# Feed-forward first stages of a two-block transformer: one 512-column product for both parts of h, sums in two banks

## The chip, the cores and the metric

The kernel runs on one core of one Trainium2 chip. The metric is the device time of one execution in microseconds. Before the change three runs gave 1700.32, 1704.14 and 1704.25 us; their median, 1704.14 us, is the time before.

## The reference, cut to what matters

x is 256 tokens by 1024 features. A first block (two attentions, then a gated feed-forward with a convolution, here called the stage "o") is followed by two layers of a second block. Each layer has a feed-forward, a mixer of three attentions, and a second feed-forward, all with modulated norms. The four feed-forwards of the two layers are what the change is about:

```
def swiglu(h, w_gate, w_up, w_down):
    return (jax.nn.silu(h @ w_gate) * (h @ w_up)) @ w_down

for l in range(DEPTH_2):                      # 2 layers
    h = modulate(x, norm_pre[l, 0], mod[:, 0, 0], mod[:, 0, 1])
    x = residual_add(x, swiglu(h, ffn_w_gate[l, 0], ffn_w_up[l, 0], ffn_w_down[l, 0]), ...)
    ...                                       # token mixer
    h = modulate(x, norm_pre[l, 2], mod[:, 2, 0], mod[:, 2, 1])
    x = residual_add(x, swiglu(h, ffn_w_gate[l, 1], ffn_w_up[l, 1], ffn_w_down[l, 1]), ...)
```

w_gate and w_up are 1024 by 2816, w_down is 2816 by 1024. All data is float32.

## The kernel before

Every product is made of float32r parts. A weight w is split into hi (a rounded copy) and lo (w minus hi), an activation h into h_hi and h_lo, and `three` (L516) adds up hi times h_hi, hi times h_lo and lo times h_hi in PSUM; lo times h_lo is left out.

The weights come in 269 chunks of 128 x 2048 (1 MB), in an order fixed beforehand. SP loads each into one of three raw buffers once the lo split of three chunks before is done (`load_chunk`, L426). ACT writes hi (`split`, L916), DVE writes lo (L1307). There are three hi/lo slots, and a fourth from the end of one mixer to the start of the next, so that in the changed stages the split of chunk k+4 stands behind the products of chunk k on ACT and on DVE (`split_behind`, L933 and L1313). A second list, 192 rows of modulation weights (ada, 0.5 MB each), is loaded by SP into three buffers and reduced on DVE, one row behind most chunks (`ada`, L1328).

A first stage of a feed-forward ("up0" and "up2" of layers 0 and 1) has 22 chunks (FT). A chunk k holds two tiles of 128 output features, j = 0 for the gate and j = 1 for the up weights, each with eight tiles t of 128 input features. Chunks 0 and 1 are done by `fm_first` (L542), which starts while h is still being made. Chunks 2 to 21 are done by `fm` (L529): 48 products with a stationary 128x128 piece of the weights and a moving 128x256 piece of h. Both j go to one bank of the pair lin, columns 0 to 255 and 256 to 511; banks alternate by chunk, and a bank is written again when DVE has signalled taken_v for the chunk two before.

```
for j in range(2):
    for t in range(KT):
        b = slice((j * KT + t) * P, (j * KT + t + 1) * P)
        ins = three(out[:, j * SEQ:(j + 1) * SEQ], hi[s][:, b], lo[s][:, b], h_hi[:, t, :],
                    h_lo[:, t, :], t == 0, t == KT - 1)
```

ACT takes Silu of the gate half out of the bank into a work tile (`silu_gate`, L1158), then makes the next hi split. DVE multiplies that with the up half (L1655; this frees the bank), makes the lo split, and writes act_hi (a rounding copy, L1647) and act_lo (L1649) with drains between (`swiglu`, L1651; `second_of`, L1645); then comes the ada row. work[2] and work[3] serve in turn.

The second stage of a feed-forward (`down`, L729) multiplies act with w_down in 11 chunks of 24 products with 512 columns (L694), into the four att banks. `into_h` (L752) turns x through pt, nps and two att banks before each first stage. Stage o.up of the first block has the same products as up0 (`fm`), but a convolution on ACT and DVE (`conv_glu`, L1666), act_hi on ACT (L1199) and act_lo on DVE (L1682); its order of work is written out by hand as well.

PSUM has eight banks here: lin 0 and 1, att 2 to 5, pt 6, nps 7.

Of the kernel before, what the change touches and what calls it, by code (L numbers as in the profile page):

```python
# [7 lines left out]
F32 = mybir.dt.float32  # L8
# [4 lines left out]
P = 128  # L13
# [186 lines left out]
def program(nc, d, known):  # L200

    with ExitStack() as ctx:
        def sb(name, shape, dt=F32, scope=ctx):
            return scope.enter_context(nc.sbuf_tensor(name, shape, dt))
# [6 lines left out]

        x = sb("x", [P, 2, D])
        sb("h_shift", [P, 72])
        h_parts = [sb("h_hi", [P, KT * SEQ + IN_STEP], F32R)]
        ada_out = sb("ada_out", [P, ADA_ALL])
        eps = sb("eps", [P, 1])
        h_parts.append(sb("h_lo", [P, KT * SEQ + IN_STEP], F32R))
        sb("work_shift", [P, 16])
        h_hi, h_lo = (h[:, 0:KT * SEQ].rearrange("p (t n) -> p t n", t=KT) for h in h_parts)
        m_hi, m_lo = (h[:, IN_STEP:].rearrange("p (t n) -> p t n", t=KT) for h in h_parts)  # L220
# [51 lines left out]
        with ExitStack() as scope:  # L272
            sb("under_fourth", [P, 56 * 256 + FOURTH_SHIFT], F32, scope)
            hi.append(sb("hi3", [P, CH], F32R, scope))
            lo.append(sb("lo3", [P, CH], F32R, scope))

        lin = ctx.enter_context(nc.psum_tensor("lin", [P, 2, 512], F32))
        att = ctx.enter_context(nc.psum_tensor("att", [P, 4, 512], F32))
        pt = ctx.enter_context(nc.psum_tensor("pt", [P, 512], F32))
# [6 lines left out]
        def signal(name):  # L286
            signals[name] = Signal(ctx.enter_context(nc.semaphore(name)), name, known)
            return signals[name]
# [27 lines left out]
                                                   signal("sp"), signal("d"))  # L316
        s_part_v, s_h, s_x = signal("part_v"), signal("h"), signal("x_made")
        s_z, s_scaled, s_h_hi_v = signal("z"), signal("scaled"), signal("h_hi_v")
        s_glu, s_half_mean = signal("glu"), signal("half_mean")
        s_act, s_taps, s_merged, s_rot, s_lat = (signal("act_made"), signal("taps"), signal("merged"), signal("rot"),  # L320
                                                 signal("lat_made"))
        s_lat_lo, s_halved = signal("lat_lo"), signal("halved")
# [86 lines left out]

        def bank_of(unit):  # L410
            return att[:, 2, :] if unit == WIDE else lin[:, BANK[unit], :]

        def ada_slot(h):

# [98 lines left out]
        def _(eng):  # L513
# [15 lines left out]
            def fm(name):  # L529

                c = AT[name]
                eng.wait_ge(*s_lo.at(c))
                out = free_bank((c, 0))
                s = SLOT[c]
                for j in range(2):
                    for t in range(KT):
                        b = slice((j * KT + t) * P, (j * KT + t + 1) * P)
                        ins = three(out[:, j * SEQ:(j + 1) * SEQ], hi[s][:, b], lo[s][:, b], h_hi[:, t, :],
                                    h_lo[:, t, :], t == 0, t == KT - 1)
                ins.then_inc(*s_mm.up((c, 0), c))  # L540

            def fm_first(tag, *names):  # L542
# [349 lines left out]
            for l in map(str, range(LAYERS)):  # L892
                into_h(l + ".pre0", flat_f, 8 if l == "0" else 5, 8 if l == "0" else 4)
                fm_first(l + ".pre0", f"{l}.up0.0", f"{l}.up0.1")
                for k in range(2, FT):
                    fm(f"{l}.up0.{k}")
                down(l + ".down0")
                into_h(l + ".pre1", flat_f, 5, 4)
                fm_first(l + ".pre1", f"{l}.moba.q0", f"{l}.moba.k0")
                tm(f"{l}.moba.v0")  # L900
                fm(f"{l}.moba.q1")
                eng.wait_ge(*s_dcon_in.at("dcon"))
                mixing(l, MIX_HEADS, MIX_SLOTS, {11: lambda: latent_sums(l)})
                out_proj(l)
                into_h(l + ".pre2", rb[:, 0:8, :], 5, 4)
                fm_first(l + ".pre2", f"{l}.up2.0", f"{l}.up2.1")
                for k in range(2, FT):
                    fm(f"{l}.up2.{k}")
                down(l + ".down2")


# [1 line left out]
        def _(eng):  # L913
# [19 lines left out]
            def split_behind(name):  # L933

                for c in SPLIT_BEHIND.get(AT[name], []):
                    if SLOT_BEFORE[c] == AT[name]:
                        split(c)
# [191 lines left out]
            def mixing(l, heads, before, slots, early, first, late):  # L1129
                n = len(heads)  # L1130
                last = 1 if l == "o" else 2
                for s in range(len(slots) + 1):
# [22 lines left out]
                    for f in late.get(s, []):  # L1155
                        f()

            def silu_gate(stage, k):  # L1158
                c = AT[f"{stage}.{k}"]
                eng.wait_ge(*s_mm.at((c, 0)))  # L1160
                act(work[2 + k % 2][:, 0:SEQ], lin[:, BANK[(c, 0)], 0:SEQ], ACT.Silu).then_inc(*s_gated.up((stage, k)))  # L1161

            def down(stage):

# [31 lines left out]
            h_first("norm2", 24, "o.1", 8)  # L1196
            split_behind("o.out.2")
            split_behind("o.out.3")
            def act_first(k):  # L1199
                eng.wait_ge(*s_glu.at(k))  # L1200
                act(act_hi[:, k, :], work[2 + k % 2][:, SEQ:2 * SEQ], ACT.Copy).then_inc(*s_act_hi.up(k))

            for k in range(FT):
                c = AT[f"o.up.{k}"]
                eng.wait_ge(*s_mm.at((c, 0)))
                for j in range(2):
                    at = PCOL["conv"].start + 8 * k + 4 * j
                    ins = act(work[k % 2][:, j * SEQ:(j + 1) * SEQ], bank_of((c, 0))[:, j * SEQ:(j + 1) * SEQ],
                              ACT.Identity, bias=par[:, at + 3:at + 4], scale=par[:, at + 1:at + 2])
                ins.then_inc(*s_conved.up(k))  # L1210
                if k:
                    act_first(k - 1)
                split_behind(NAMES[c])
                eng.wait_ge(*s_taps.at(k))
                act(work[2 + k % 2][:, 0:SEQ], work[k % 2][:, SEQ:2 * SEQ], ACT.Gelu_apprx_tanh).then_inc(
                    *s_gated.up(("o.up", k)))
            eng.wait_ge(*s_cond_b_in.at(1))
            act(cs[:], cs[:], ACT.Silu).then_inc(*s_silu.up(1))
            act_first(FT - 1)
            log_exp()  # L1220
            down("o.down")
            factor_of_x("norm3", "down", 0)
# [4 lines left out]
            for l in map(str, range(LAYERS)):  # L1227
# [2 lines left out]
                split_behind("o.down.10" if l == "0" else "0.down2.10")  # L1230
                for k in range(FT):
                    silu_gate(l + ".up0", k)
                    split_behind(f"{l}.up0.{k}")

                log_exp()
                down(l + ".down0")
# [50 lines left out]
                split_behind(f"{l}.out.3")  # L1287
                for k in range(FT):
                    silu_gate(l + ".up2", k)
                    split_behind(f"{l}.up2.{k}")  # L1290
                log_exp()
                down(l + ".down2")
                if l == "0":
# [8 lines left out]
        def _(eng):  # L1302
# [10 lines left out]
            def split_behind(name):  # L1313

                for c in SPLIT_BEHIND.get(AT[name], []):
                    if SLOT_BEFORE[c] == AT[name]:
                        split(c)
# [324 lines left out]
                        o_second(l, h + 1)  # L1642
                    ada(c)

            def second_of(k, stage, a):  # L1645

                ve.tensor_copy(act_hi[:, k, :], a)  # L1647
                ve.drain()
                tt(act_lo[:, k, :], a, act_hi[:, k, :].bitcast(F32), ALU.subtract).then_inc(*s_act.up((stage, k)))  # L1649

            def swiglu(stage, to, k):  # L1651
                c = AT[f"{stage}.{k}"]
                w = work[2 + k % 2]
                eng.wait_ge(*s_gated.at((stage, k)))
                tt(w[:, SEQ:2 * SEQ], w[:, 0:SEQ], lin[:, BANK[(c, 0)], SEQ:2 * SEQ], ALU.mult).then_inc(  # L1655
                    *s_taken_v.up((c, 0)))
                split_behind(NAMES[c])
                ve.drain()
                second_of(k, to, w[:, SEQ:2 * SEQ])
                ada(c)  # L1660

            def conv_glu(k):
                c = AT[f"o.up.{k}"]
                eng.wait_ge(*s_conved.at(k))
                for j in (1, 0):
                    at = PCOL["conv"].start + 8 * k + 4 * j  # L1666
                    u = work[k % 2][:, j * SEQ:(j + 1) * SEQ]
                    p = bank_of((c, 0))[:, j * SEQ:(j + 1) * SEQ]
                    stt(u[:, 1:SEQ], p[:, 0:SEQ - 1], par[:, at:at + 1], u[:, 1:SEQ], ALU.mult, ALU.add)
                    ve.drain()  # L1670
                    ins = stt(u[:, 0:SEQ - 1], p[:, 1:SEQ], par[:, at + 2:at + 3], u[:, 0:SEQ - 1], ALU.mult, ALU.add)  # L1671
                    ins.then_inc(*(s_taps.up(k) if j else s_taken_v.up((c, 0))))
                split_behind(NAMES[c])
                if k:
                    act_second(k - 1)
                ve.drain()  # L1676
                eng.wait_ge(*s_gated.at(("o.up", k)))
                w = work[2 + k % 2]
                tt(w[:, SEQ:2 * SEQ], w[:, 0:SEQ], work[k % 2][:, 0:SEQ], ALU.mult).then_inc(*s_glu.up(k))
                ada(c)  # L1680

            def act_second(k):  # L1682

                eng.wait_ge(*s_act_hi.at(k))
                tt(act_lo[:, k, :], work[2 + k % 2][:, SEQ:2 * SEQ], act_hi[:, k, :].bitcast(F32),
                   ALU.subtract).then_inc(*s_act.up(("o.down", k)))

            eng.wait_ge(*s_silu.at(0))
            for i, h in enumerate(START_ORDER):
# [33 lines left out]
            for k in range(FT):  # L1723
                conv_glu(k)
                if k == 15:
                    gate_of(40, "down")
            act_second(FT - 1)
            for k in range(FD - 1):
                if k < FD - 2:
                    split_behind(f"o.down.{k}")  # L1730
# [27 lines left out]
            for l in map(str, range(LAYERS)):  # L1758
# [2 lines left out]
                split_behind("o.down.10" if l == "0" else "0.down2.10")  # L1761
                for k in range(FT):
                    swiglu(l + ".up0", l + ".down0", k)
                layer_post(l, 0)
                for k in range(FD - 1):
                    c = AT[f"{l}.down0.{k}"]
# [29 lines left out]
                split_behind(f"{l}.out.3")  # L1796
                for k in range(FT):
                    swiglu(l + ".up2", l + ".down2", k)
                layer_post(l, 2)
                for k in range(FD - 1):  # L1800
                    c = AT[f"{l}.down2.{k}"]
# [206 lines left out]
```

## Time and profile before

| | |
|---|---|
| median of three runs | 1704.14 us |
| the profiled execution | 1706.34 us |
| its span, first to last instruction | 1704.5 us |
| mean granted clock of TensorE | 0.997 of full speed |
| instructions | 29606, of them 12344 products |

PE is TensorE's products, PEld its weight loads, DVE VectorE, ACT ScalarE, POOL GpSimd, SP the engine that issues most DMAs. "SPq" is a queue, "lin", "att", "work" and the like are the program's names, L with a number is a line of the kernel before. Spans of products overlap, so the time from one start to the next, not the shown length, is what a product costs in a stream; some product records can be missing. "x945" is a number of instructions, "<-" in brackets names what an engine waited for.

### The profile page before, as it was taken

The page shows a single profiled execution, that of the slowest core. Times are in us where ns is not written, and L with a number is a line of the kernel's source. Part 1 is how long each engine was busy: PE and PEld are TensorE (multiplying, and loading weights), DVE is VectorE, ACT ScalarE, POOL GpSimd, SP SyncE. Part 2 cuts the span into 40 slices and gives each one's busy share as a digit, 9 for nine tenths or more (in the row PEclk, how much of TensorE's full clock was granted, in tenths as well). Part 3 has the DMA queues.
Part 4 walks back from the last instruction along what each step waited for, and adds up shares of the span by engine and source line. Part 5 has one row for each costly group of instructions (what it writes and reads, how often), then busy time and mean ns, then how long its engine had stood idle before and what let it go on. Part 6 is the DMA issues. An engine that isn't in the chain of part 4 may idle for free.

```text
span 1704.5 us, 29606 instructions
## 1 busy us (share of the span) xinstructions
PE 1661.0 (97%) x12344; PEld 1551.7 (91%) x12344; DVE 1266.7 (74%) x1852; ACT 873.3 (51%) x1214; POOL 21.7 (1%) x39
## 2 busy tenths in 40 slices
PE   3999999998999999999999999999999999999998
PEld 3999899987999899989989998999899989989997
DVE  7777889977877677776878775877677776878553
ACT  4565466653534355676373434533355676473432
POOL 0000000000000000000000000000000000000000
PEclk9999999999999999999999999999999999999999
DMA  9878756777677744756548786687945856547542
GB/s 378 314 259 249 275 195 213 203 293 280 258 292 276 287 169 184 223 178 232 207 177 296 272 220 261 227 292 270 289 170 183 220 181 233 210 174 259 196 167 96
DMA packets 71078, 398.80 MB, mean 234 GB/s; under 512 B 8224, under 2 KB 8736, under 8 KB 36384
## 3 DMA queue, kind: packets, MB, share of 16 engines
q1 hardware_dynamic: 67968, 387.43, 65.1%
q0 software_dynamic: 2976, 9.47, 1.6%
q8 instruction: 98, 1.61, 0.4%
q14 instruction: 36, 0.29, 0.0%
HBM read 395.79 MB, written 1.08 MB: 233 GB/s over the span
## 4 chain that ended last, share of the span: by engine, by line
PE 79%; DVE 7%; ACT 5%; DMA 4%; DVEq 3%; issue 1%; SPq 1%; ACTq 0%
PE lin L517 18%; PE lin L518 17%; PE lin L519 17%; PE att L694 15%; DVE lo L1310 4%; ACT hi L921 3%; PE att L801 2%; PE lin L557 1%; DMA raw<-in_w 1%; PE lin L559 1%; PE lin L567 1%; DMA ada_w<-in_ada 1%; DVEq L1676 1%; PE att L851 1%; DMA ada_s<-in_ada 1%
## 5 line engine op out<-in xcount | busy, mean ns | idle before, releaser
L1310 DVE TENSOR_TENSOR lo<-raw,hi 128x2048 fp32r<-128x2048 f32 x269 | 615.6, 2291 | 253.1 <-ACT hi L921 252.4
L517 PE MATMUL lin<-h_hi,hi 128*128 128x256 f32 x2448 | 688.5, 281 | 1.3 <-DVE work L1671 0.8
L518 PE MATMUL lin<-h_lo,hi 128*128 128x256 f32 x2448 | 683.8, 279 | 0.0
L519 PE MATMUL lin<-h_hi,lo 128*128 128x256 f32 x2448 | 682.5, 279 | 0.0
L921 ACT ACTIVATE hi<-raw 128x2048 fp32r<-128x2048 f32 x269 | 513.5, 1912 | 194.8 <-PE att L694 91.4
L517 PEld LDWEIGHTS lin<-h_hi,hi 128*128 128x128 f32 x2448 | 460.0, 188 | 4.0 <-issue 3.8
L518 PEld LDWEIGHTS lin<-h_lo,hi 128*128 128x128 f32 x2448 | 460.3, 188 | 0.1
L519 PEld LDWEIGHTS lin<-h_hi,lo 128*128 128x128 f32 x2448 | 460.1, 188 | 0.0
L1323 DVE CUSTOM_DVE_ANT_0 ada_w<-ada_w,cs 128x1024 f32<-128x1024 f32 x179 | 218.0, 1219 | 18.8 <-DMA ada_w<-in_ada 18.7
L1161 ACT ACTIVATE work<-lin 128x256 f32<-128x256 f32 x88 | 33.9, 386 | 269.4 <-PE lin L519 268.2
L694 PE MATMUL att<-hi,act_hi 128*128 128x512 f32 x440 | 138.8, 389 | 0.0
L694 PE MATMUL att<-lo,act_hi 128*128 128x512 f32 x440 | 138.7, 389 | 0.0
L694 PE MATMUL att<-hi,act_lo 128*128 128x512 f32 x440 | 138.7, 389 | 0.0
L694 PEld LDWEIGHTS att<-lo,act_hi 128*128 128x128 f32 x440 | 82.6, 188 | 17.2
L694 PEld LDWEIGHTS att<-hi,act_lo 128*128 128x128 f32 x440 | 82.6, 188 | 17.2
L694 PEld LDWEIGHTS att<-hi,act_hi 128*128 128x128 f32 x440 | 82.2, 188 | 16.8
L517 PE MATMUL lin<-br_hi,hi 128*128 128x256 f32 x224 | 63.4, 283 | 0.1
L518 PE MATMUL lin<-br_lo,hi 128*128 128x256 f32 x224 | 62.5, 279 | 0.0
L519 PE MATMUL lin<-br_hi,lo 128*128 128x256 f32 x224 | 62.5, 279 | 0.0
L557 PE MATMUL lin<-h_hi,hi 128*128 128x256 f32 x224 | 53.4, 282 | 1.1 <-ACT h_hi L1006 1.1
L517 PE MATMUL lin<-hi,h_hi 128*128 128x256 f32 x192 | 54.2, 283 | 0.0
L519 PE MATMUL lin<-hi,h_lo 128*128 128x256 f32 x192 | 53.9, 281 | 0.0
(291 smaller groups left out, 2023.7 us busy)
## 6 DMA issues: line engine op xcount, KB each, us to landing
raw<-in_w SPq DMA_DIRECT2D x269, 1024.0 KB, 4.9
ada_w<-in_ada SPq DMA_DIRECT2D x179, 512.0 KB, 5.4
ada_s<-in_ada SPq DMA_DIRECT2D x13, 512.0 KB, 15.3
bias<-in_bias POOLq DMA_DIRECT2D x16, 256.0 KB, 4.4
ffn_row<-rows POOLq DMA_DIRECT2D x5, 512.0 KB, 9.1
x<-in_x SPq DMA_DIRECT2D x1, 1024.0 KB, 9.6
ra<-rows POOLq DMA_DIRECT2D x2, 512.0 KB, 5.0
dcon<-in_dcon SPq DMA_DIRECT2D x1, 896.0 KB, 8.0
```

Of the source, the lines that this page charges most:

```text
L517: mm(out, w_hi, a_hi, start=start, stop=False, skip_group_check=skip)
L518: mm(out, w_hi, a_lo, start=False, stop=False, skip_group_check=skip)
L519: return mm(out, w_lo, a_hi, start=False, stop=stop, skip_group_check=skip)
L557: mm(o, hi[SLOT[c]][:, b], h_hi[:, t, :], start=t == 0 and j == 0, stop=False, skip_group_check=True)
L559: mm(o, lo[SLOT[c]][:, b], h_hi[:, t, :], start=False, stop=False, skip_group_check=True)
L567: ins = mm(outs[i][:, j * SEQ:(j + 1) * SEQ], hi[SLOT[c]][:, b], h_lo[:, t, :], start=False, stop=t == 3, skip_group_check=True)
L694: ins = mm(att[:, 2 * a + n, :], act[:, t, tokens], w[s][:, kk * D + n * 512:kk * D + (n + 1) * 512], start=t == 0 and i == 0, stop=t == 2 ...
L801: ins = mm(out, q, k, start=start, stop=stop, skip_group_check=skip)
L921: act(hi[SLOT[c]][:], raw[:, c % RAW, :], ACT.Copy).then_inc(*s_hi.up(c))
L1161: act(work[2 + k % 2][:, 0:SEQ], lin[:, BANK[(c, 0)], 0:SEQ], ACT.Silu).then_inc(*s_gated.up((stage, k)))
L1310: tt(lo[SLOT[c]][:], raw[:, c % RAW, :], hi[SLOT[c]][:].bitcast(F32), ALU.subtract).then_inc(*s_lo.up(c))
L1323: ve.tensor_tensor_reduce(out=w, in0=w, in1=cs[:], scale=1.0, scalar=0.0, op0=ALU.mult, op1=ALU.add, accum_out=ada_out[:, h:h + 1]).then_i ...
```

## The change

In chunks 2 to 21 of the four first stages (`fm_apart` in place of `fm`), hi is multiplied with h_hi and h_lo in one product of 512 columns, and lo with h_hi in one of 256: 32 products for 48. The 512 columns of a bank hold, for one j, the sum of hi times h_hi and lo times h_hi (columns 0 to 255) and hi times h_lo (256 to 511). j = 0 and 1 have a bank each: banks 0 and 1 for odd k, 6 and 7 (pt, nps) for even k. ACT copies both second halves out (a new wait on act_made and a new signal, low), DVE adds the first halves (this frees the banks), ACT takes Silu in SBUF, DVE multiplies. act_hi moves from DVE to ACT and act_lo to one chunk later, as o.up has it. On DVE the ada row now comes ahead of the lo split. h_both is a tile laid over h_hi, ada_out, eps and h_lo, whose places stay. The diff leaves out the same lines for up2, and in o.up the new names of act_first, act_second and the label of glu.

```diff
@@ -211,10 +211,13 @@
 
         x = sb("x", [P, 2, D])
         sb("h_shift", [P, 72])
-        h_parts = [sb("h_hi", [P, KT * SEQ + IN_STEP], F32R)]
+        with ExitStack() as place:
+            h_both = sb("h_both", [P, 2, KT * SEQ + IN_STEP + ADA_ALL + 1], F32R, place)
+        sb("h_hi_place", [P, KT * SEQ + IN_STEP], F32R)
         ada_out = sb("ada_out", [P, ADA_ALL])
         eps = sb("eps", [P, 1])
-        h_parts.append(sb("h_lo", [P, KT * SEQ + IN_STEP], F32R))
+        sb("h_lo_place", [P, KT * SEQ + IN_STEP], F32R)
+        h_parts = [h_both[:, i, 0:KT * SEQ + IN_STEP] for i in range(2)]
         sb("work_shift", [P, 16])
         h_hi, h_lo = (h[:, 0:KT * SEQ].rearrange("p (t n) -> p t n", t=KT) for h in h_parts)
         m_hi, m_lo = (h[:, IN_STEP:].rearrange("p (t n) -> p t n", t=KT) for h in h_parts)
@@ -274,6 +277,8 @@
             hi.append(sb("hi3", [P, CH], F32R, scope))
             lo.append(sb("lo3", [P, CH], F32R, scope))
 
+        with ExitStack() as place:
+            banks = place.enter_context(nc.psum_tensor("banks", [P, 8, 512], F32))
         lin = ctx.enter_context(nc.psum_tensor("lin", [P, 2, 512], F32))
         att = ctx.enter_context(nc.psum_tensor("att", [P, 4, 512], F32))
         pt = ctx.enter_context(nc.psum_tensor("pt", [P, 512], F32))
@@ -316,7 +321,7 @@
                                                    signal("sp"), signal("d"))
         s_part_v, s_h, s_x = signal("part_v"), signal("h"), signal("x_made")
         s_z, s_scaled, s_h_hi_v = signal("z"), signal("scaled"), signal("h_hi_v")
-        s_glu, s_half_mean = signal("glu"), signal("half_mean")
+        s_low, s_glu, s_half_mean = signal("low"), signal("glu"), signal("half_mean")
         s_act, s_taps, s_merged, s_rot, s_lat = (signal("act_made"), signal("taps"), signal("merged"), signal("rot"),
                                                  signal("lat_made"))
         s_lat_lo, s_halved = signal("lat_lo"), signal("halved")
@@ -409,6 +414,9 @@
 
         def bank_of(unit):
             return att[:, 2, :] if unit == WIDE else lin[:, BANK[unit], :]
+
+        def pair_of_banks(k):
+            return banks[:, 0:2, :] if k % 2 else banks[:, 6:8, :]
 
         def ada_slot(h):
 
@@ -537,6 +545,24 @@
                         b = slice((j * KT + t) * P, (j * KT + t + 1) * P)
                         ins = three(out[:, j * SEQ:(j + 1) * SEQ], hi[s][:, b], lo[s][:, b], h_hi[:, t, :],
                                     h_lo[:, t, :], t == 0, t == KT - 1)
+                ins.then_inc(*s_mm.up((c, 0), c))
+
+            def fm_apart(name):
+
+                c = AT[name]
+                eng.wait_ge(*s_lo.at(c))
+                k = int(name.split(".")[-1])
+                if k > 2:
+                    eng.wait_ge(*s_taken_v.at((c - 2, 0)))
+                s = SLOT[c]
+                for j in range(2):
+                    out = pair_of_banks(k)[:, j, :]
+                    for t in range(KT):
+                        b = slice((j * KT + t) * P, (j * KT + t + 1) * P)
+                        mm(two(out), hi[s][:, b], h_both[:, :, t * SEQ:(t + 1) * SEQ], start=t == 0, stop=False,
+                           skip_group_check=True)
+                        ins = mm(out[:, 0:SEQ], lo[s][:, b], h_hi[:, t, :], start=False, stop=t == KT - 1,
+                                 skip_group_check=True)
                 ins.then_inc(*s_mm.up((c, 0), c))
 
             def fm_first(tag, *names):
@@ -893,7 +919,7 @@
                 into_h(l + ".pre0", flat_f, 8 if l == "0" else 5, 8 if l == "0" else 4)
                 fm_first(l + ".pre0", f"{l}.up0.0", f"{l}.up0.1")
                 for k in range(2, FT):
-                    fm(f"{l}.up0.{k}")
+                    fm_apart(f"{l}.up0.{k}")
                 down(l + ".down0")
                 into_h(l + ".pre1", flat_f, 5, 4)
                 fm_first(l + ".pre1", f"{l}.moba.q0", f"{l}.moba.k0")
...
@@ -1155,10 +1181,27 @@
                     for f in late.get(s, []):
                         f()
 
+            def act_first(stage, k):
+                eng.wait_ge(*(s_taken_v.at((AT[f"{stage}.{k}"], 0)) if stage != "o.up" and k < 2 else
+                              s_glu.at((stage, k))))
+                act(act_hi[:, k, :], work[2 + k % 2][:, SEQ:2 * SEQ], ACT.Copy).then_inc(*s_act_hi.up((stage, k)))
+
             def silu_gate(stage, k):
                 c = AT[f"{stage}.{k}"]
-                eng.wait_ge(*s_mm.at((c, 0)))
-                act(work[2 + k % 2][:, 0:SEQ], lin[:, BANK[(c, 0)], 0:SEQ], ACT.Silu).then_inc(*s_gated.up((stage, k)))
+                w = work[2 + k % 2]
+                if k < 2:
+                    eng.wait_ge(*s_mm.at((c, 0)))
+                    act(w[:, 0:SEQ], lin[:, BANK[(c, 0)], 0:SEQ], ACT.Silu).then_inc(*s_gated.up((stage, k)))
+                    split_behind(NAMES[c])
+                else:
+                    eng.wait_ge(*s_mm.at((c, 0)))
+                    eng.wait_ge(*s_act.at((stage.replace("up", "down"), k - 2)))
+                    act(two(w), pair_of_banks(k)[:, :, SEQ:2 * SEQ], ACT.Copy).then_inc(*s_low.up((stage, k)))
+                    split_behind(NAMES[c])
+                    eng.wait_ge(*s_taken_v.at((c, 0)))
+                    act(w[:, 0:SEQ], w[:, 0:SEQ], ACT.Silu).then_inc(*s_gated.up((stage, k)))
+                if k:
+                    act_first(stage, k - 1)
 
             def down(stage):
 
...
@@ -1230,7 +1269,7 @@
                 split_behind("o.down.10" if l == "0" else "0.down2.10")
                 for k in range(FT):
                     silu_gate(l + ".up0", k)
-                    split_behind(f"{l}.up0.{k}")
+                act_first(l + ".up0", FT - 1)
 
                 log_exp()
                 down(l + ".down0")
...
@@ -1642,22 +1681,32 @@
                         o_second(l, h + 1)
                     ada(c)
 
-            def second_of(k, stage, a):
-
-                ve.tensor_copy(act_hi[:, k, :], a)
-                ve.drain()
-                tt(act_lo[:, k, :], a, act_hi[:, k, :].bitcast(F32), ALU.subtract).then_inc(*s_act.up((stage, k)))
+            def act_second(stage, to, k):
+
+                eng.wait_ge(*s_act_hi.at((stage, k)))
+                tt(act_lo[:, k, :], work[2 + k % 2][:, SEQ:2 * SEQ], act_hi[:, k, :].bitcast(F32),
+                   ALU.subtract).then_inc(*s_act.up((to, k)))
 
             def swiglu(stage, to, k):
                 c = AT[f"{stage}.{k}"]
                 w = work[2 + k % 2]
+                if k < 2:
+                    eng.wait_ge(*s_gated.at((stage, k)))
+                    tt(w[:, SEQ:2 * SEQ], w[:, 0:SEQ], lin[:, BANK[(c, 0)], SEQ:2 * SEQ], ALU.mult).then_inc(
+                        *s_taken_v.up((c, 0)))
+                    split_behind(NAMES[c])
+                    if k:
+                        act_second(stage, to, k - 1)
+                    ada(c)
+                    return
+                eng.wait_ge(*s_low.at((stage, k)))
+                tt(two(w), two(w), pair_of_banks(k)[:, :, 0:SEQ], ALU.add).then_inc(
+                    *s_taken_v.up((c, 0)))
+                ada(c)
+                split_behind(NAMES[c])
                 eng.wait_ge(*s_gated.at((stage, k)))
-                tt(w[:, SEQ:2 * SEQ], w[:, 0:SEQ], lin[:, BANK[(c, 0)], SEQ:2 * SEQ], ALU.mult).then_inc(
-                    *s_taken_v.up((c, 0)))
-                split_behind(NAMES[c])
-                ve.drain()
-                second_of(k, to, w[:, SEQ:2 * SEQ])
-                ada(c)
+                tt(w[:, SEQ:2 * SEQ], w[:, 0:SEQ], w[:, SEQ:2 * SEQ], ALU.mult).then_inc(*s_glu.up((stage, k)))
+                act_second(stage, to, k - 1)
 
             def conv_glu(k):
                 c = AT[f"o.up.{k}"]
...
@@ -1761,6 +1804,7 @@
                 split_behind("o.down.10" if l == "0" else "0.down2.10")
                 for k in range(FT):
                     swiglu(l + ".up0", l + ".down0", k)
+                act_second(l + ".up0", l + ".down0", FT - 1)
                 layer_post(l, 0)
                 for k in range(FD - 1):
                     c = AT[f"{l}.down0.{k}"]
...
```

## Rows read from the trace of the kernel before

**Rows 1.** The page, part 1: busy time of each engine, share of the span, instructions

```profile
PE 1661.0 (97%) x12344; PEld 1551.7 (91%) x12344; DVE 1266.7 (74%) x1852; ACT 873.3 (51%) x1214; POOL 21.7 (1%) x39
```

**Rows 2.** Windows: stretch, its us, busy us of engines, PEclk, DMA share, GB/s

```profile
440.00:550.00 110.00, 110.00 (x945) 110.00 (x944) 89.97 (x119) 44.05 (x41) 0.00 (x0) 1.00 0.83 305
```

**Rows 3.** The chain that ended last, by time: start us, us, what

```profile
436.13 3.73 PE lin L567 x32
...
551.92 59.90 PE att L694 x264
...
883.98 3.77 PE lin L567 x32
1000.81 59.87 PE att L694 x264
...
1074.68 3.77 PE lin L567 x32
1191.51 59.87 PE att L694 x264
...
1522.97 3.73 PE lin L567 x32
1638.78 59.87 PE att L694 x264
```

**Rows 4.** Timeline of ACT, then DVE: start, us, operation [idle before, releaser]

```profile
456.76 0.39 ACT L1161 ACTIVATE work<-lin 128x256 f32<-128x256 f32 x1 [3.41 <-PE lin L519]
457.04 1.91 ACT L921 ACTIVATE hi<-raw 128x2048 fp32r<-128x2048 f32 x1
...
457.63 0.42 DVE L1655 TENSOR_TENSOR work<-work,lin 128x256 f32<-128x256 f32 x1
458.99 2.29 DVE L1310 TENSOR_TENSOR lo<-raw,hi 128x2048 fp32r<-128x2048 f32 x1 [0.94 <-ACT hi L921]
...
462.08 1.22 DVE L1323 CUSTOM_DVE_ANT_0 ada_w<-ada_w,cs 128x1024 f32<-128x1024 f32 x1
...
463.23 0.42 DVE L1655 TENSOR_TENSOR work<-work,lin 128x256 f32<-128x256 f32 x1
```

**Rows 5.** Groups by line and shape: busy us, mean ns | idle before, releaser

```profile
L1061 ACT ACTIVATE lat<-lin 128x512 f32<-128x512 f32 x2 | 1.2, 599 | 3.7 <-PE lin L519 3.7
...
L1437 DVE TENSOR_TENSOR flat_f<-att,ffn_row 128x512 f32<-128x512 f32 x20 | 13.6, 686 | 18.0 <-PE att L694 15.7 <-ACT work L941 2.0
...
L1647 DVE CAST act_hi<-work 128x256 fp32r<-128x256 f32 x88 | 26.0, 295 | 8.0
```

**Rows 6.** Timeline of the o.up stage, DVE, then ACT

```profile
259.65 2.29 DVE L1310 TENSOR_TENSOR lo<-raw,hi 128x2048 fp32r<-128x2048 f32 x1 [0.39 <-ACT hi L921]
261.86 0.42 DVE L1685 TENSOR_TENSOR act_lo<-work,act_hi 128x256 fp32r<-128x256 f32 x1
262.37 0.43 DVE L1679 TENSOR_TENSOR work<-work 128x256 f32<-128x256 f32 x1
262.71 0.48 DVE L1669 SCALAR_TENSOR_TENSOR work<-lin,par,work 128x255 f32<-128x255 f32 x1
...
265.09 2.29 DVE L1310 TENSOR_TENSOR lo<-raw,hi 128x2048 fp32r<-128x2048 f32 x1 [0.39 <-ACT hi L921]
...
262.83 0.42 ACT L1201 ACTIVATE act_hi<-work 128x256 fp32r<-128x256 f32 x1 [1.96 <-DVE work L1679]
263.16 1.90 ACT L921 ACTIVATE hi<-raw 128x2048 fp32r<-128x2048 f32 x1
```

**Rows 7.** Timeline, start of the first changed stage: ACT, then DVE

```profile
441.89 1.92 ACT L921 ACTIVATE hi<-raw 128x2048 fp32r<-128x2048 f32 x1 [1.39 <-DMA raw<-in_w]
...
443.85 2.29 DVE L1310 TENSOR_TENSOR lo<-raw,hi 128x2048 fp32r<-128x2048 f32 x1
```

**Rows 8.** Timeline of the same stretch: issues on SP's queue

```profile
446.17 0.33 SPq L429 DMA_DIRECT2D raw<-in_w  x1
...
448.20 0.33 SPq L434 DMA_DIRECT2D ada_w<-in_ada  x1
```

More of the change, by code:

```diff
@@ L907, in _ @@
                 for k in range(2, FT):
-                    fm(f"{l}.up2.{k}")
+                    fm_apart(f"{l}.up2.{k}")
                 down(l + ".down2")
@@ L1198, in _ @@
             split_behind("o.out.3")
-            def act_first(k):
-                eng.wait_ge(*s_glu.at(k))
-                act(act_hi[:, k, :], work[2 + k % 2][:, SEQ:2 * SEQ], ACT.Copy).then_inc(*s_act_hi.up(k))
             for k in range(FT):
@@ L1211, in _ @@
                 if k:
-                    act_first(k - 1)
+                    act_first("o.up", k - 1)
                 split_behind(NAMES[c])
@@ L1218, in _ @@
             act(cs[:], cs[:], ACT.Silu).then_inc(*s_silu.up(1))
-            act_first(FT - 1)
+            act_first("o.up", FT - 1)
             log_exp()
@@ L1289, in _ @@
                     silu_gate(l + ".up2", k)
-                    split_behind(f"{l}.up2.{k}")
+                act_first(l + ".up2", FT - 1)
                 log_exp()
@@ L1674, in conv_glu @@
                 if k:
-                    act_second(k - 1)
+                    act_second("o.up", "o.down", k - 1)
                 ve.drain()
@@ L1678, in conv_glu @@
                 w = work[2 + k % 2]
-                tt(w[:, SEQ:2 * SEQ], w[:, 0:SEQ], work[k % 2][:, 0:SEQ], ALU.mult).then_inc(*s_glu.up(k))
+                tt(w[:, SEQ:2 * SEQ], w[:, 0:SEQ], work[k % 2][:, 0:SEQ], ALU.mult).then_inc(*s_glu.up(("o.up", k)))
                 ada(c)
[L1682 to L1686, printed above, removed]
             eng.wait_ge(*s_silu.at(0))
@@ L1726, in _ @@
                     gate_of(40, "down")
-            act_second(FT - 1)
+            act_second("o.up", "o.down", FT - 1)
             for k in range(FD - 1):
@@ L1798, in _ @@
                     swiglu(l + ".up2", l + ".down2", k)
+                act_second(l + ".up2", l + ".down2", FT - 1)
                 layer_post(l, 2)
```

## The prediction

> **What bounds the kernel now.** I read the page's engine shares first: PE is busy 97% of the span, DVE 74%, ACT 51% [rows 1]. A share is an average over stages, so I then asked for one changed stage by itself. In 440 to 550 us (the first feed-forward of layer 0) PE and its weight loads are busy for all of the 110 us, at a granted clock of 1.00, which is the upper level, 2.4 GHz; DVE has 90 us of work, ACT 44, and the DMA engines stand at 0.83 [rows 2]. So a shorter product stream shortens this stage, until DVE and ACT become the limit.
>
> Third, the chain that ended last, which gives the exact length of the four changed stages and the pace of both sorts of product [rows 3]. A stage's chunks 2 to 21 run from the end of the L567 piece to the start of the L694 piece: 551.92-439.86 = 112.06 us, then 113.06, 113.06 and 112.08; 450.26 in all. That is 20 chunks of 48 products of 256 columns, so 116.7 ns each in the outer two stages and 117.8 in the inner two. A down stage is 264 products of 512 columns in 59.87 to 59.90 us, 226.8 ns each. The 256 further columns cost 226.8-116.7 = 110.1 ns, near the 106.7 that one column a cycle of 2.4 GHz would give; by that estimate a 256-column product carries 10 to 11 ns beside its columns, a 512-column one 13.5. Two of 256 cost 6.6 ns more than one of 512 (2x116.7-226.8), 8.8 at the slower pace. This is what the change can win.
>
> Fourth, one period of ACT and DVE in that stage [rows 4]: Silu waits 3.41 us for PE, the product that frees the bank ends 1.3 us after Silu began, and DVE's lo split waits 0.94 us for ACT's hi split. Both engines follow PE, with room.
>
> **The change, part by part.**
>
> *Products.* A chunk's 48 products become 16 of 512 and 16 of 256 columns, as many columns as before. One chunk: 16x(226.8+116.7) = 5.50 us against 5.60 to 5.65. A stage: 109.92 us; four: 439.7 against 450.26, a gain of 10.6 us if the 256-column products run at 116.7, and 9.9 if they keep 117.8 in the inner stages. I take 10.2. No row shows a moving operand in two pieces (h_hi and h_lo lie apart), nor these two lengths in turn, so the 512-column product is bounded: 223.3 ns if its cost beside the columns is the 10.0 of a 256-column one (another 1280x3.5 = 4.5 us gained), 233.4 if each piece costs a whole product of its own (nothing gained). I take 226.8, the nearest row: same data type, same columns, as many weight loads for each product.
>
> The rows give 6.6 ns for what one product fewer saves [rows 3]. The Trainium skill, TensorE: Matmul & The Clock Gate, Back-to-back issue gap, has a warm isolated product at its columns over 2.4 GHz plus about 2.5 ns; by it the 1280 merged products would save an estimated 3.2 us, where the rows give 10.
>
> *Weight loads* fall by 1280 with the products; they lie beside them.
>
> *Evacuation.* A chunk now fills two banks, in turn lin and pt/nps. Each pair is used again at every second chunk, as each bank was, so PE may still run one chunk ahead. pt and nps were last read to make h, for which fm_first waits already; chunk 2 loses its wait, worth nothing, as PE stands still nowhere in rows 2. Per chunk ACT adds a 512-element Copy out of PSUM, 0.60 us by a like row, and act_hi's Copy, 0.42 (from DVE, where it was a cast of 0.30 and two drains); DVE gets the add of 512 elements out of PSUM, 0.69, beside mult 0.43 and subtraction 0.42 [rows 5, 6]. These close a ring that did not exist: Copy(k) waits for act_second(k-2), the last thing of swiglu(k-1), as both use the same work tile. Behind Copy on ACT stand the next hi split, Silu and act_first; DVE waits for it with the add, and behind that stand ada, the lo split, mult and act_second. So neither engine can run ahead, and the ring's period counts.
>
> I work it out from starts that rows show: an ACT or DVE instruction begins some 0.1 before its predecessor's shown end (2.21 after the start of lo, 0.34 after that of mult [rows 6], 0.28 after Silu's, 1.15 after ada's [rows 4]), and a hand-over costs 0.03 to 0.04 either way [rows 6]. From Copy's start: hi starts at 0.50 and ends at 2.41; lo starts at 2.45, mult at 4.66, act_second at 5.00, which ends at 5.42; the next Copy starts at 5.46. DVE's other branch, add at 0.64 and ada at 1.25, is free at 2.40, so ada hides under hi, and chunks without one are no faster. Thus 5.46 against PE's 5.50: PE stays the limit by a hair. The ring of o.up tests such sums: lo to lo 5.44, of pieces 2.21+0.51+0.46+0.33+1.93 [rows 6].
>
> The hair matters little, because the banks give slack. PE gets a pair back 1.37 us after Copy starts (0.64+0.69+0.04) and needs it 5.50 after the chunk ended: Copy may be 4.1 late. At the stage's start hi(5) waits for its DMA until 441.89, lo follows at 443.85 [rows 7], act_second(0) ends at 446.48 and Copy(2) starts at 446.52, 1.2 late on PE's 439.86+5.50; the next is 1.4 late, as ada(1) stands before its add. So 2.7 us are left over 18 chunks: the ring may take 5.65 before PE waits at all. With Copy between 0.56 (twice the Silu's 0.28) and 0.70, and an add of up to 0.80, the ring takes 5.42 to 5.62. Cost: 0 at both ends.
>
> *Order on the queues.* ada goes ahead of the lo split on DVE. SP issued raw at the end of lo, and ada_w 2.03 us later at the end of ada [rows 8]; now ada's buffer is free before lo ends, so the two loads go out together. Each still has more than two periods, 11 us, until it is needed; I cost it at nothing. The cover is the three buffers of each, and if it went, a late load would hold the ring, and PE only past those 2.7 us. The names in o.up and the joint tile over h's old addresses change no instruction there. At a stage's end the two last act_second lie under 60 us of down products.
>
> **Sum.** The profiled execution took 1706.34 us, its span 1704.5: less 10.2 it is 1696.1. The median shown, 1704.14, is 2.2 below that execution, so I predict 1694. About 0.3%, 5.1 us, is what a measurement here can tell from no change; the term is twice that.
>
> **Rivals.**
> A, no gain to speak of: the operand in two pieces pays its start twice, 230 to 233.4 ns. For it: no row has such an operand. Against it: in all rows the fixed part goes with the instruction. Gain 0 to 4.4 us (1280x3.4): 1700 to 1704. The 2.5 ns of the Trainium skill (the section above) would land there as well.
> B, slower: the ring becomes the limit. Place: Copy's wait for act_second. Price: past 5.65 each 0.1 us costs 18x0.1x4 = 7.2 us. It eats the gain at 5.79 and is slower by over 5.1 us from 5.86, 0.40 above my sum; at 6.0 it makes +15, 1719. For it: 5.46 against 5.50 is close, and stray stalls of an engine would add. Against it: every piece has a row, and o.up's ring fits its pieces.
> C, more: the weights of the 256-column product load under the longer one, and its 10 ns beside the columns vanish: at most 1280x10 = 12.8 us more, 1681; half of it is likelier, 1688. For it: weight loads fill the changed stage wholly [rows 2]. Against it: the 512-column stream has 13.5 ns though its loads have twice the time.
>
> **Chances.** Forecast 0.73 (own range 1689 to 1699), A 0.12, B 0.08, C 0.07. Faster by over 0.3%: forecast and C, less the forecast's tail, 0.78. Within it: A and that tail, 0.13. Slower: B and a little noise of A, 0.09. The range for 8 in 10 takes in the forecast and most of A: 1688 to 1703.
>
> **What will show it.** In the changed profile the four stages should be 109.9 to 110.3 us between the same two marks, PE without idle time in them; the 512- and 256-column products spaced so that a pair takes some 343 ns; Copy starting 1 to 2 us after PE's last product of the chunk, steady along the stage; lo waiting for hi in every chunk. Wrong: pairs of 350 (A) or 330 (C), or PE waiting for the add, with Copy's lateness growing to 4 us (B).

## The result, and the profile after

The changed kernel takes 1706.54 us, the median of 20 runs, against 1703.7 before, also of 20: a ratio of 1.0015, 95% interval 1.0009 to 1.0021. It was forecast at 1694 and is a little slower than before.

The two profiled executions must not be set side by side by their spans. That of after (1701.5 us, execution 1703.25) was the fastest of its 20 runs, that of before (1704.5 and 1706.34) slower than all of its 20. Up to the first mark of the chain they differ by 4.4 us (436.13 [rows 3] against 431.70), and in the eleven profiles below that mark lies anywhere from 429.8 to 435.8 us. Most of the 4.4 stands in four waits for transfers ahead of the mark: 36.4 us together before, 33.5 after. Behind the mark the stages of one profile agree to a few hundredths or fall on two paces, so stages are compared between marks.

The chain that ended last, after (start us, us, what), answers to [rows 3]:

```profile
431.70 3.94 PE lin L593 x32
547.86 59.87 PE att L720 x264
...
880.64 3.94 PE lin L593 x32
996.79 59.87 PE att L720 x264
1070.59 3.93 PE lin L593 x32
...
1186.73 54.43 PE att L720 x240
...
1519.57 3.94 PE lin L593 x32
1635.73 59.87 PE att L720 x264
```

All four stages now take 112.2 us (547.86-435.64 and so on), 448.9 together against 450.3: 1.4 us gained where 10.2 were forecast. A pair of products, one of 512 and one of 256 columns, takes 112.22/320 = 350.7 ns, not 343.4. There is a second sign: the 32 last products of fm_first, which the diff does not touch, take 3.94 us instead of 3.73 to 3.78. The mixers, also untouched, took 258.15 and 257.66 us before (mark to mark of fm_first) and take 258.9 and 258.95. The four such pieces ahead of the changed stages and the two mixers (each of which begins with one more such piece) cost 2.8 us more, which turns the gain of 1.4 into a loss of 1.4 from the first mark to the end (1701.5-431.70 against 1704.5-436.13). The other 1.4 of the 2.8 between the medians is not settled: the part ahead of that mark scatters by more.

PE's starts in a changed stage, after (timeline: start us, us, operation):

```profile
469.49 0.39 PE L562 MATMUL banks<-h_both,hi 128*128 128x512 f32 x1
469.72 0.28 PE L564 MATMUL banks<-h_both,lo 128*128 128x256 f32 x1
469.84 0.40 PE L562 MATMUL banks<-h_both,hi 128*128 128x512 f32 x1
470.07 0.28 PE L564 MATMUL banks<-h_both,lo 128*128 128x256 f32 x1
```

The 512-column product holds PE for 0.23 us and the other for 0.12; by the starts of a whole stage it is 233.7 and 117.0 ns, so the longer one takes 6.9 ns more than forecast, and merging saves nothing against two products at 116.7. PE has no idle time here: from 440 to 540 us it is busy for all of the 100, at a granted clock of 1.00. ACT and DVE were not the cause (timeline of ACT, then of DVE; what ended the idle time stands in brackets):

```profile
447.86 0.60 ACT L1199 ACTIVATE work<-banks 128x512 f32<-128x512 f32 x1 [2.75 <-DVE act_lo L1687]
453.36 0.60 ACT L1199 ACTIVATE work<-banks 128x512 f32<-128x512 f32 x1 [2.48 <-DVE act_lo L1687]
...
491.82 0.60 ACT L1199 ACTIVATE work<-banks 128x512 f32<-128x512 f32 x1 [2.48 <-PE banks L564]
...
448.49 0.69 DVE L1703 TENSOR_TENSOR work<-work,banks 128x512 f32<-128x512 f32 x1 [0.72 <-ACT work L1199]
...
450.30 2.29 DVE L1349 TENSOR_TENSOR lo<-raw,hi 128x2048 fp32r<-128x2048 f32 x1
452.51 0.42 DVE L1708 TENSOR_TENSOR work<-work 128x256 f32<-128x256 f32 x1
452.84 0.42 DVE L1687 TENSOR_TENSOR act_lo<-work,act_hi 128x256 fp32r<-128x256 f32 x1
```

Copy waits for act_lo as foretold, and its starts lie 5.50 us apart (453.36-447.86; summed beforehand: 5.46). PE's period is 5.61, so the ring catches up, and at 491.82 Copy waits for PE instead.

### The profile page after: what moved, and what is told of

Its sections match the earlier page's. It is cut to its first block, busy times and chain, and to the rows that moved or that the text cites. A ratio compares the mean times of both kernels' runs of the same rounds, so it can differ in the third digit from the quotient of the medians.

```text
span 1701.5 us, 27106 instructions
## 1 busy us (share of the span) xinstructions
PE 1662.5 (98%) x11064; PEld 1495.4 (88%) x11064; DVE 1285.2 (76%) x1844; ACT 941.4 (55%) x1382; POOL 21.8 (1%) x39
## 4 chain that ended last, share of the span: by engine, by line
PE 78%; DVE 8%; ACT 5%; DMA 3%; DVEq 3%; issue 1%; SPq 1%; ACTq 0%
PE banks L562 18%; PE att L720 14%; PE banks L564 9%; PE lin L525 9%; PE lin L526 9%; PE lin L527 9%; DVE lo L1349 4%; ACT hi L947 3%; PE att L827 2%; PE lin L583 1%; PE lin L593 1%; DMA raw<-in_w 1%; PE lin L585 1%; DMA ada_w<-in_ada 1%; DVEq L1725 1%
## 5 line engine op out<-in xcount | busy, mean ns | idle before, releaser
L562 PE MATMUL banks<-h_both,hi 128*128 128x512 f32 x1280 | 449.0, 395 | 0.0
L564 PE MATMUL banks<-h_both,lo 128*128 128x256 f32 x1280 | 357.4, 279 | 0.0
L526 PE MATMUL lin<-h_both,hi 128*128 128x256 f32 x1168 | 330.4, 283 | 0.0
L525 PE MATMUL lin<-h_both,hi 128*128 128x256 f32 x1168 | 328.3, 281 | 0.5 <-DVE work L1720 0.5
L527 PE MATMUL lin<-h_both,lo 128*128 128x256 f32 x1168 | 326.2, 279 | 0.0
L562 PEld LDWEIGHTS banks<-h_both,hi 128*128 128x128 f32 x1280 | 240.3, 188 | 58.0
L564 PEld LDWEIGHTS banks<-h_both,lo 128*128 128x128 f32 x1280 | 240.3, 188 | 0.0
L525 PEld LDWEIGHTS lin<-h_both,hi 128*128 128x128 f32 x1168 | 219.5, 188 | 2.9 <-issue 2.6
L527 PEld LDWEIGHTS lin<-h_both,lo 128*128 128x128 f32 x1168 | 220.6, 189 | 0.0
L526 PEld LDWEIGHTS lin<-h_both,hi 128*128 128x128 f32 x1168 | 218.6, 187 | 0.1
L1199 ACT ACTIVATE work<-banks 128x512 f32<-128x512 f32 x80 | 47.9, 599 | 204.2 <-PE banks L564 108.7
L1703 DVE TENSOR_TENSOR work<-work,banks 128x512 f32<-128x512 f32 x80 | 55.1, 688 | 59.8 <-ACT work L1199 59.8
```

What stands on the lines that cost most here:

```text
L525: mm(out, w_hi, a_hi, start=start, stop=False, skip_group_check=skip)
L526: mm(out, w_hi, a_lo, start=False, stop=False, skip_group_check=skip)
L527: return mm(out, w_lo, a_hi, start=False, stop=stop, skip_group_check=skip)
L562: mm(two(out), hi[s][:, b], h_both[:, :, t * SEQ:(t + 1) * SEQ], start=t == 0, stop=False, skip_group_check=True)
L564: ins = mm(out[:, 0:SEQ], lo[s][:, b], h_hi[:, t, :], start=False, stop=t == KT - 1, skip_group_check=True)
L1199: act(two(w), pair_of_banks(k)[:, :, SEQ:2 * SEQ], ACT.Copy).then_inc(*s_low.up((stage, k)))
```

## The experiments

Why does a 512-column product cost as much as two? The first clue is fm_first's piece: same lines, same products, slower, and all 32 of its products read h_lo. The tiles' addresses say where h_lo went. Before, the tile eps of 4 bytes takes up 32, and h_lo starts 9216 bytes (2304 floats) behind h_hi; h_both counts eps as one float, so its second part starts 9188 bytes (2297 floats) behind the first, 28 bytes lower. The document said ahead of the prediction that the places stay; for h_lo that is not so.

**h_lo back in its place** (e1_aligned).

```diff
-            h_both = sb("h_both", [P, 2, KT * SEQ + IN_STEP + ADA_ALL + 1], F32R, place)
+            h_both = sb("h_both", [P, 2, KT * SEQ + IN_STEP + ADA_ALL + 8], F32R, place)
```

> The changed kernel with one constant altered: the stride between the two parts in h_both is 2304 floats instead of 2297, so that h_lo lies where it lay before the change (in the changed kernel it lies 28 bytes lower, since the 4-byte tile eps takes 32). Theory P (place): reading h_lo from its new place is what costs, 7.0 ns per 512-column product (233.7 against 226.7) and 6.4 ns for each of the 32 last products of fm_first (123.1 against 116.7). Then a 512-column product takes 226.7 ns, a pair 343.4, each of the four stages 109.9 us, the L593 pieces 3.73 us again, and the median falls to about 1694 (ratio to before 0.994). Theory A of the prediction (each piece of a two-piece operand pays a start of its own): the product stays at 233.4, a pair at 350, the stages at 112.2 us, the time at 1703 to 1706. Theory M (lengths that alternate cost more, because the load of the next weights lies under the shorter one): as A, pair at 350.

Measured: 1697.66 us, ratio to before 0.9967 (0.9955 to 0.9979). Two of the four stages in the chain (the others are alike):

```profile
433.63 3.73 PE lin L593 x32
548.30 59.87 PE att L720 x264
...
1068.14 3.73 PE lin L593 x32
1182.81 54.43 PE att L720 x240
```

Each stage takes 110.94 us, a pair 346.7 ns, fm_first's piece 3.73 us again (3.77 in the last stage), the mixers 257.6 and 257.7. One constant is worth 8.9 us between the medians of two sets of runs and 8.5 from the first mark to the end of the two profiles, and with it the change is a gain. But the pair stops halfway: 346.7, not 343.4.

**The place alone, without the merged product** (e2_before_moved): the kernel before, with h_hi and h_lo laid out as in the changed kernel.

```diff
-        h_parts = [sb("h_hi", [P, KT * SEQ + IN_STEP], F32R)]
+        with ExitStack() as place:
+            h_both = sb("h_both", [P, 2, KT * SEQ + IN_STEP + ADA_ALL + 1], F32R, place)
+        sb("h_hi_place", [P, KT * SEQ + IN_STEP], F32R)
...
+        h_parts = [h_both[:, i, 0:KT * SEQ + IN_STEP] for i in range(2)]
```

> The kernel before with nothing changed but the place of h_lo: it is put 28 bytes lower, as in the changed kernel; all products are those of before. Theory P: every product that reads h_lo suffers; the L567 pieces take 3.94 us instead of 3.73, and a chunk's 48 products, of which 16 move h_lo, take up to 16x6.4 = 0.10 us more, 5.70 instead of 5.60, stages of up to 114 us; over all first stages, gates and projections the time rises by 3 us (if it shows as little as in the mixers of the changed kernel, 0.4 ns a product) to 16 us (2448 products at 6.4 ns). Theories A and M: stages of 112.1 and 113.1 us as before, time as before within 2 us.

Measured: 1709.72 us, ratio 1.0034 (1.0022 to 1.0047), slower with not one product changed. The chain, first and third stage:

```profile
432.71 3.92 PE lin L570 x32
549.71 59.90 PE att L697 x264
...
1073.71 3.94 PE lin L570 x32
1190.73 59.90 PE att L697 x264
```

All four stages take 113.08 us. Now the two parts of the diff can be told apart, by the sum of the four stages in us:

| | h_lo in its old place | 28 bytes lower |
|---|---|---|
| three products of 256 | 450.26 | 452.32 |
| one of 512, one of 256 | 443.76 | 448.86 |

Merging gains 6.5 us in the old place and 3.5 in the new one; the move costs 2.1 us in these stages without merging and 5.1 with it, and 3 us more in fm_first and the mixers either way. The table holds one profile for each cell, and one cell is a mixture: before, with h_lo in its old place, has two stages at 112.07 and two at 113.06 us. With four alike it would hold 448.3 or 452.2, so how much of the 6.5 and of the 2.1 belongs to the edit is open by up to 2 us either way; the three other cells have all four stages within 0.02 us of each other.

**Other places of h_lo** (e3_off32, e4_off16, e7_off64): the constant 16, 12 and 24 in place of 8.

> As e1_aligned, but with the stride 8 floats longer: h_lo lies at 32 past a multiple of 64 bytes. Theory P with a grain of 32 bytes: 226.7 ns and L593 pieces of 3.73 us as in e1_aligned; with a grain of 64: near 233.7 and 3.94. Theories A and M: 233.7 in any place.

> As e1_aligned, but with the stride 4 floats longer: h_lo lies at 16 past a multiple of 64 bytes. Theory P with a grain of 32 or 64 bytes: 233.7 ns and L593 pieces of 3.94 us; with a grain of 16: 226.7 and 3.73. Theories A and M: 233.7 in any place.

> e1_aligned with the stride 16 floats longer: h_lo 64 bytes past its old place. Theory P with a grain of 64 bytes: 228.3 and 118.3 ns as in e1_aligned, stages of 110.9 us. If not the place within 64 bytes but this one place were right: 233 or more, as in e3_off32 and e4_off16.

Chains of e3 (two stages):

```profile
434.69 3.63 PE lin L593 x32
550.33 59.89 PE att L720 x264
...
883.26 3.77 PE lin L593 x32
1000.08 59.87 PE att L720 x264
```

of e4:

```profile
434.27 3.78 PE lin L593 x32
551.12 59.87 PE att L720 x264
```

of e7:

```profile
431.93 3.83 PE lin L593 x32
546.70 59.87 PE att L720 x264
```

32 bytes off, a pair takes 350.0 or 353.3 ns (112.01 or 113.05 us), 16 off 353.3; 64 off it is 346.7 again (110.94). A single time each: 1706.96, 1707.78 and 1697.85 us. So for the merged products only the place modulo 64 bytes counts, as far as these places show it. The untouched products don't follow the same rule: 32 off, fm_first's piece takes 3.63 or 3.77 us, about as before or faster, while the mixers are slower (259.1); 64 off the piece is slower (3.83), as are the mixers (258.9). "A misplaced operand is slow" is too simple.

**One piece instead of two** (e5_one_piece): h_hi(t) and h_lo(t) side by side.

```diff
-                        mm(two(out), hi[s][:, b], h_both[:, :, t * SEQ:(t + 1) * SEQ], start=t == 0, stop=False,
+                        mm(out, hi[s][:, b], h_both[:, 2 * t * SEQ:2 * (t + 1) * SEQ], start=t == 0, stop=False,
```

> The changed kernel with h kept by tile: h_hi(t) and h_lo(t) lie side by side, each at a multiple of 64 bytes, so that the 512 columns of a product are one run and not two pieces. All else is that of the changed kernel. With h_lo back in its place (e1_aligned) a 512-column product still took 228.3 ns and the pair 346.7, not the 226.7 and 343.4 that the rows of before gave. Theory A in what is left of it (a second piece costs 1.6 ns and as much on the next product): here 226.7 and 116.7, a pair of 343.4, stages of 109.9 us, about 4 us less than e1_aligned (1693.5). Theory P alone (only the places of what is read count): near 346.7 and 1697.7, unless the new places of the h tiles happen to be better or worse by a few ns. Theory M (lengths in turn): 346.7.

Its chain, first stage:

```profile
432.55 3.73 PE lin L591 x32
547.23 59.87 PE att L718 x264
```

110.95 us, the pair 346.7 as in e1. A second piece costs nothing; rival A's mechanism is wrong, although its price, 233.4 ns, was almost the measured one. The two lengths, by the starts, share the pair out differently from stage to stage: 226.8 and 120.0 ns in the first stage of e5, 228.4 and 118.3 in the second and third, 230.0 and 116.7 in the fourth (what was expected of e9 gives only 228.3 and 118.3). Each of the two prices of the forecast occurs, but never both in one stage. The kernel takes 1696.97 us, ratio 0.9963 (0.9949 to 0.9976), with e1 the best of all.

**The lengths apart** (e6_lengths_apart): in each bank the eight long products first, then the eight short ones.

```diff
                     for t in range(KT):
...
                         mm(two(out), hi[s][:, b], h_both[:, :, t * SEQ:(t + 1) * SEQ], start=t == 0, stop=False,
                            skip_group_check=True)
+                    for t in range(KT):
+                        b = slice((j * KT + t) * P, (j * KT + t + 1) * P)
                         ins = mm(out[:, 0:SEQ], lo[s][:, b], h_hi[:, t, :], start=False, stop=t == KT - 1,
```

> e1_aligned with another order of the products in a bank: first the eight of 512 columns, then the eight of 256. Theory M: without the change of length from one product to the next they take 226.7 and 116.7 ns, 343.4 together, stages of 109.9 us, 4 us less than e1_aligned. Theories A and P: 346.7 as in e1_aligned, stages of 110.9 us, time within 1.5 us of e1_aligned.

```profile
433.59 3.73 PE lin L595 x32
549.33 59.88 PE att L722 x264
```

112.01 us (112.27 in the third stage), 350.0 a pair, and 1701.27 us (0.9986, 0.9976 to 0.9995): worse than in turn. The loss is with the long ones (PE's timeline, eight products a row):

```profile
469.83 1.09 PE L566 MATMUL banks<-h_both,lo 128*128 128x256 f32 x8
470.76 2.03 PE L562 MATMUL banks<-h_both,hi 128*128 128x512 f32 x8
472.63 1.09 PE L566 MATMUL banks<-h_both,lo 128*128 128x256 f32 x8
```

By the starts eight short ones take 0.93 us, 116 ns each, and eight long ones 1.87, 234 each. Changing lengths are not what costs. The same products on the same data, at the same addresses, run 3.3 ns a pair slower in another order, in which other weights are loaded beside each. That points to the loads, without showing it.

**The weights moved, h left alone** (e8_weights_moved; of the other tiles between, ada_w and x move too, which these products do not read).

```diff
-        sb("weight_shift", [P, 56])
+        sb("weight_shift", [P, 48])
...
-        sb("h_shift", [P, 72])
+        sb("h_shift", [P, 80])
```

> e1_aligned with hi and lo of slots 0 to 2 moved 32 bytes down (to a multiple of 64 bytes; before they were 32 past one), h in its place. Theory P, first form (the place of the moving operand alone counts): 228.3 and 118.3 ns in the three slots as in the fourth, which is not moved, stages of 110.9 us. Second form (the place of h against that of the weights counts, as the weights are read beside it): another pace, of 233 or more for the 512-column product, in the chunks of slots 0 to 2, the pace of e1_aligned in those of the fourth.

PE's timeline over two chunks of the first stage, first and last row of 16 and of 14 long products; the first chunk's weights lie in the fourth slot, which was not moved, the second's in a moved one:

```profile
456.20 0.39 PE L562 MATMUL banks<-h_both,hi 128*128 128x512 f32 x1
...
461.40 0.39 PE L562 MATMUL banks<-h_both,hi 128*128 128x512 f32 x1
...
462.09 0.40 PE L562 MATMUL banks<-h_both,hi 128*128 128x512 f32 x1
...
466.68 0.40 PE L562 MATMUL banks<-h_both,hi 128*128 128x512 f32 x1
```

(461.40-456.20)/15 = 346.7 ns a pair with the unmoved weights, (466.68-462.09)/13 = 353.1 with the moved ones, in one stage, with h in one place. It is so in all four stages: the chunks of the fourth slot stay at 346 to 348, those of the others at 352 to 354; only the first chunk of the second stage lies between, at 348.8. So where the weights lie counts too, and not the place of h alone. The down stages, whose moving operand is these weights, change too, from 59.87 to 61.24 us:

```profile
429.76 3.77 PE lin L593 x32
545.96 61.24 PE att L720 x264
```

The single time is 1705.82 us.

**All of h moved** (e9_h_plus16, e10_h_plus48, e11_h_plus32): e5 with an offset into its tile of 4, 12 and 8 floats.

> e5_one_piece with both parts of h 16 bytes higher; the weights stay. What is open: e1_aligned and e5_one_piece take 228.3+118.3 = 346.7 ns a pair where the sum of the forecast had 226.7+116.7 = 343.4. Theory P in its second form (place of h against the weights, modulo 64 bytes; e8_weights_moved bore it out): a pair other than 346.7; if it comes to 343.4 or less, the residue is of the same sort. As h_lo alone 16 higher cost 353.3 (e4_off16), I expect 350 or more here, stages of 112 us and up. If pairs stay at 346.7, the place of h_hi does not count and the second form is wrong.

> e5_one_piece with both parts of h 48 bytes higher (16 lower modulo 64). Theory P, second form: a pair other than 346.7; h_lo alone 28 lower cost 350.7 (the changed kernel), so 348 to 353, or 343.4 if this is the good place. First form: 346.7 cannot hold either, as the place modulo 64 changes; so this run and e9_h_plus16 only scan for a better place.

> e5_one_piece with both parts of h 32 bytes higher. Slots 0 to 2 of the weights and h then stand to each other as in e8_weights_moved (there the weights were 32 lower), where the pair took 353.3 ns in those slots and 346.6 in the fourth; here the fourth slot stands so too. Theory P, second form: 353 ns in the chunks of all four slots, stages of 113.0 us. First form (the place of h alone): no such tie to e8_weights_moved.

The first stages of e9,

```profile
435.81 3.79 PE lin L591 x32
551.60 59.89 PE att L718 x264
```

of e10,

```profile
433.61 3.84 PE lin L591 x32
550.50 59.87 PE att L718 x264
```

and of e11:

```profile
434.13 3.63 PE lin L591 x32
550.82 59.87 PE att L718 x264
```

112.0, 113.05 and 113.06 us; a single time each of 1707.92, 1711.53 and 1705.84 us (before, beside them, 1699.88, also single). e11 gives 353.3 ns, the number that e8 had foretold from moving the weights the other way: it is the place of one against the other that counts. With h in four places 16 bytes apart, the old place is the best by 3.3 ns a pair, and 343.4 appears in none.

## Why the prediction was wrong, point by point

*The four marked stages are limited by PE*: right, before, after and in all variants: PE is busy for all of the 110 us that were looked at in each stage.

*"... the joint tile over h's old addresses change no instruction there"*: this step failed, and the sum has no term for it. No instruction changed, but the tile did not lie over the old addresses; h_lo sank by 28 bytes. That cost 5.1 us in the stages and about 3 in products that the diff does not touch; e1 gives all of it back.

*A pair as the sum of two prices, 226.8 and 116.7 ns*: the second step that failed. The first price came from the down stages, "same data type, same columns, as many weight loads for each product", and was given bounds; the second was taken over without any. In the best place found the pair takes 346.7, so the term was about 6.5 us and not 10.2. Of e5's four stages one has its long products at the forecast 226.8, and there the short ones take 120.0; the one with short ones at 116.7 has long ones at 230.0. Why no stage has both stays open. The rows had a warning: the same 48 products took 116.7 ns in two stages and 117.8 in two [rows 3], and I averaged over what I could not explain. The kernel before had another: weight_shift, h_shift and work_shift are tiles that nothing reads, and all that they do is to move the tiles behind them.

*The Trainium skill's rule*: the Trainium skill's 2.5 ns beside the columns of a warm isolated product (TensorE: Matmul & The Clock Gate, Back-to-back issue gap) gave an estimated 3.2 us. The runs gave 3.5 us in the one place and 6.5 in the other, 2.7 and 5.1 ns for each of 1280; neither that figure nor the row's 6.6 ns holds by itself.

*The ring*: 5.46 summed, 5.50 measured, Copy's lateness shrinking as PE's period is longer; B did not happen. At the forecast 343.4 ns a pair PE's period would have been 5.49 us, so the hair of room was not there; only the slack of the banks was. *The queues*: in each changed stage ACT or DVE waits for a transfer just once, at its start, 1.15 to 1.34 us; before it was 1.21 to 1.39. *Rival A*: its price fitted, its cause did not (e5), and it knew nothing of the 3 us in other stages, so the time came out above its 1704. *Rival C*: the pair never went below 346.7.

*The range* left out the end that came true, since I let a gain be eaten but no untouched product slow down.

## What to carry to other kernels

Where an edit merges or re-lays tiles, print the addresses before and after: a tile of 4 bytes took 32, and the 28 bytes decided the sign of the change. A product's price in a stream belongs to the places of its two operands and to the products beside it, so a row from another stage bounds it but does not give it; when untouched products change their pace, look for a moved operand first. Measure the edit in a two by two table, each part with and without the other.

## What the runs showed of the hardware

The pace of float32r products depends on where the weights lie against the moving operand, modulo 64 bytes for the merged ones: 346.7, 350.0 to 350.7 or 353.3 ns a pair in all the places tried. Place is not all: e6 has every address of e1, and another order of the products makes 350.0 of 346.7. The Trainium skill, TensorE: Matmul & The Clock Gate, Step-by-step: what each phase is for, says that loading the next weights takes no read bandwidth from the running product. By that one would not expect e8: of all that these products read, only the weights moved, and it costs 6.4 ns a pair, and in the fourth slot, unmoved, nothing. The measurement decides; whether read bandwidth is what is lost, no run shows.

One place can also have two paces: 350.2 and 353.3 in before, 350.0 and 353.3 in e3, each held through a whole stage. In both kernels the pace goes with fm_first's piece just ahead of the stage (3.73 with 350.2, 3.77 with 353.3; in e3 3.63 with 350.0, 3.77 with 353.3), so it seems to be picked before the stage begins; but in e11 the pieces differ in the same way as in e3, and all four stages take 353.3. What picks one, why the paces are these, and whether a pair of 343.4 exists for some other place, stays open.
